# The first layer's attention, issued item by item beside the weight chunks instead of as a stage of its own

## The reference, cut to what matters

```python
def even_mixer(h, w_in, lq1, lk1, lq2, lk2, sub_g, sinks, w_out, lambda_init):
    proj = h @ w_in                      # 2048 -> 4352
    qa, ka, va, qs, ks, vs = jnp.split(proj, idx, axis=-1)
    a_out = diff_attention(qa, ka, va, lq1, lk1, lq2, lk2, sub_g, lambda_init)
    b_out = swa_with_sinks(qs, ks, vs, sinks)
    return jnp.concatenate([a_out, b_out], axis=-1) @ w_out
```

## Time and profile before

| | us |
|---|---|
| median of three runs | 3366.43 (3366.3 to 3367.06) |
| the profiled execution's own time | 3365.45 |
| its span in the trace | 3363.7 |
| busy in it: TensorE, VectorE, ScalarE, GpSimd | 3254.8, 1887.4, 1589.8, 263.5 |

### The profile page before, as it was taken

One profiled execution on the slowest core, in us unless ns is written; L12 is line 12 of the kernel. 1 busy time (PEld: TensorE's weight loads), 2 busy tenths in 40 slices (PEclk: granted clock), 3 DMA queues, 4 the chain that ended last, 5 costly groups with the idle time before them and its releaser, 6 DMA issues.

```text
span 3363.7 us, 39873 instructions
## 1 busy us (share of the span) xinstructions
PE 3254.8 (97%) x15175; PEld 2679.0 (80%) x15175; DVE 1887.4 (56%) x2128; ACT 1589.8 (47%) x2186; POOL 263.5 (8%) x335
## 2 busy tenths in 40 slices
PE   8988999999999999999999999999989999999998
PEld 6866878888888787778888888878778888888886
DVE  4465555554555567755555555557876555554445
ACT  5445454444444467645444445553354543444343
POOL 0001000000000001000460003630000000000000
PEclk9975989999999999989999999989999999999999
DMA  6630545656565455546565556656535665665663
GB/s 229 188 111 7 187 145 189 191 186 191 187 190 185 152 182 163 170 144 200 189 192 190 188 188 218 233 183 203 168 131 168 180 190 194 190 191 189 193 192 116
DMA packets 321365, 595.44 MB, mean 177 GB/s; under 512 B 32612, under 2 KB 39828, under 8 KB 320936
## 3 DMA queue, kind: packets, MB, share of 16 engines
q1 hardware_dynamic: 321192, 593.04, 56.2%
HBM read 581.96 MB, written 11.01 MB: 176 GB/s over the span
## 4 chain that ended last, share of the span: by engine, by line
PE 89%; DVE 6%; ACT 3%; issue 1%; SPq 0%; DMA 0%; ACTq 0%; DVEq 0%
PE pair L1683 27%; PE pair L1685 27%; PE pair L1684 27%; DVE lo L1031 2%; PE turn_ps L1714 1%; ACT hi L575 1%; PE pair L1912 1%; PE turn_ps L1896 1%; PE turn_ps L1838 0%; PE pair L1985 0%; PE misc_ps L1812 0%; PE pair L1838 0%; PE pair L1986 0%; PE pair L1885 0%; DVE conv_o L1136 0%
## 5 line engine op out<-in xcount | busy, mean ns | idle before, releaser
L1031 DVE TENSOR_TENSOR lo<-raw,hi 128x1024 fp32r<-128x1024 f32 x1084 | 1340.2, 1240 | 1291.1 <-ACT hi L575 1280.4
L575 ACT ACTIVATE hi<-raw 128x1024 fp32r<-128x1024 f32 x1084 | 1144.7, 1060 | 1416.0 <-PE pair L1685 1394.2
L1683 PE MATMUL pair<-hi,xt_h 128*128 128x512 f32 (+1 forms) x2784 | 1096.6, 394 | 16.1 <-DVE lo L1031 7.1
L1685 PE MATMUL pair<-lo,xt_h 128*128 128x512 f32 (+1 forms) x2784 | 1086.1, 390 | 0.0
L1684 PE MATMUL pair<-hi,xt_l 128*128 128x512 f32 (+1 forms) x2784 | 1085.5, 390 | 0.0
L1683 PEld LDWEIGHTS pair<-hi,xt_h 128*128 128x128 f32 x2784 | 526.7, 189 | 134.2 <-DVE lo L1031 10.1
L1685 PEld LDWEIGHTS pair<-lo,xt_h 128*128 128x128 f32 x2784 | 525.9, 189 | 109.8
L1684 PEld LDWEIGHTS pair<-hi,xt_l 128*128 128x128 f32 x2784 | 526.6, 189 | 105.2
L1683 PE MATMUL pair<-hi,ht_h 128*128 128x512 f32 x1504 | 587.8, 391 | 4.9 <-DVE ht_l L1145 3.6
L1685 PE MATMUL pair<-lo,ht_h 128*128 128x512 f32 x1504 | 585.4, 389 | 0.0
L1684 PE MATMUL pair<-hi,ht_l 128*128 128x512 f32 x1504 | 585.2, 389 | 0.0
(11 more groups left out here) (279 smaller groups left out, 1745.5 us busy)
## 6 DMA issues: line engine op xcount, KB each, us to landing
raw<-in_mlp_w SPq DMA_DIRECT2D x512, 512.0 KB, 4.1
raw<-in_w_gate SPq DMA_DIRECT2D x88, 512.0 KB, 4.1
raw<-in_w_up SPq DMA_DIRECT2D x88, 512.0 KB, 4.1
raw<-in_w_down SPq DMA_DIRECT2D x88, 512.0 KB, 3.9
raw<-in_even_w_in SPq DMA_DIRECT2D x68, 512.0 KB, 4.4
raw<-in_odd_w_in SPq DMA_DIRECT2D x64, 512.0 KB, 4.0
raw<-in_w_in SPq DMA_DIRECT2D x64, 512.0 KB, 3.9
raw<-in_even_w_out SPq DMA_DIRECT2D x32, 512.0 KB, 4.1
```

The source lines that it names most:

```text
L575: nc.scalar.activation(hi[:, r], raw[:, slot], ACT.Copy).then_inc(sems["hi_ready"], 1)
L1031: nc.vector.tensor_tensor(lo[:, r], raw[:, slot], hi[:, r].bitcast(F32), ALU.subtract).then_inc(sems["lo_ready"], 1)
L1683: nc.tensor.matmul(to, xh[:, t0 + k, tok], h[:, k], start=s, stop=False)
L1685: mm = nc.tensor.matmul(to, xh[:, t0 + k, tok], l[:, k], start=False, stop=e)
```

## The change

The two calls of `attention` and the `drain` are gone. The 32 items, window items first, are issued by a new `heads_at(slot)` beside the chunks, one every second slot from slot 16 on, and one slot later from item 24 on. The input chunks run in the order 6, 8, 7, 0, 2, 4, 1, 3, 5, 68 units in slots 0 to 67. Scores are issued one slot before an item's own, then follow bias (0), exps and probabilities (1), scaling of a window item and the turn (2), copy (3), product (4), out of PSUM (5). Scores have one PSUM buffer (`pair[1]`), turns and products one bank each of `misc_ps`. A window item's probabilities are divided by their sum on ScalarE before the turn, and its product has the values as the stationary operand, so that its output has features on the partitions; it goes into `qk0` in place of its queries. Differential outputs go into `o_diff` with tokens on the partitions. Their heads are normed in three batches (four pairs, two, two): root on ScalarE, reciprocal and product on VectorE, turn on TensorE, hi and lo from PSUM with the gain `subg` as a column.

The output projection is now eight chunks of four units: four with the window half of the weights' rows, set into `acc` in slots 68 to 83, then four with the differential half, added to it. The window half waits for `split_window`, four pairs of roundings and subtractions behind the last input unit; the differential half waits for the batches in turn. Items 24 to 31 run beside the window half.

```diff
-                    64 if kind == "window" else P)
+        FIRST, OUT_WIN, OUT_DIFF = 16, 68, 84
+        HEADS = ([("window", pr, m) for pr in range(8) for m in range(M)]
+                 + [("diff", pr, m) for pr in range(8) for m in range(M)])
+        BATCHES = ((0, 4, 0), (4, 6, 0), (6, 8, 2))
+
+        def head_step(slot, after):
+            k = (slot - after - FIRST) // 2
+            if k >= 24:
+                k = (slot - after - FIRST - 1) // 2
+            late = k >= 24
+            return k if 0 <= k < 32 and FIRST + 2 * k + late + after == slot else None
+
+        def batch_step(slot, after):
+            for b, (_, end, _) in enumerate(BATCHES):
+                k = 16 + 2 * end - 1
+                if FIRST + 2 * k + (k >= 24) + 5 + after == slot:
+                    return b
+            return None
+
+        def roots(b):
+            return stat[:, SUB:SUB + 16].rearrange("p (m h) -> p m h", m=M)[:, :, BATCHES[b][0]:BATCHES[b][1]]
...
-                    self.unit(w_even_in[:, KU * k:KU * k + KU, 0:CH])
+                    self.unit(w_even_in[:, KU * k:KU * k + KU, 6 * CH:7 * CH])
                 for dst, src in (
                     (grows[0:8], i["post_mix_g"].rearrange("l (c n) -> (l c) n", n=CH)),
...
-                    (subg[:], i["even_subln_g"].partition_broadcast(P)),
+                    (subg[:], i["even_subln_g"].rearrange("a p -> p a")),
...
+            def heads_at(self, slot):
+
+                if slot == 13:
+                    self.eng.wait_ge(sems["lam_dot"], 1)
...
+                if b is not None:
+                    self.eng.wait_ge(sems["a_out"], 16 + 2 * BATCHES[b][1])
+                    nc.scalar.activation(roots(b), roots(b), ACT.Sqrt, scale=1.0 / P, bias=eps_col
+                                         ).then_inc(sems["o_root"], 1)
+                k = head_step(slot, 1)
+                if k is not None:
+                    self.head_exp(k)
+                k = head_step(slot, 2)
+                if k is not None and k < 16:
+                    self.head_scale(k)
+                b = batch_step(slot, 2)
+                if b is not None:
+                    self.batch_hi(b)
+
...
+            def head_out(self, k):
+                kind, pr, m = HEADS[k]
+                self.eng.wait_ge(sems["a_mixed"], k + 1)
+                mixed = misc_ps[:, 1, 0:P]
+                if kind == "window":
+                    a = nc.scalar.activation(qk0[:, 16 + pr, m * P:(m + 1) * P], mixed, ACT.Copy)
+                else:
+                    nc.scalar.activation(junk[:], mixed, ACT.Square, accum_out=st(SUB + 8 * m + pr))
+                    a = nc.scalar.activation(o_diff[:, m, pr * P:(pr + 1) * P], mixed, ACT.Copy)
+                a.then_inc(sems["a_out"], 1)
+
+            def batch_hi(self, b):
+                a, e, at = BATCHES[b]
+                self.eng.wait_ge(sems["o_turned"], b + 1)
+                nc.scalar.activation(xt_h[:, a:e], turn_ps[:, at:at + e - a], ACT.Copy, scale=subg[:]
+                                     ).then_inc(sems["o_hi"], 1)
+
+            def split_window(self):
+
+                self.eng.wait_ge(sems["unit_used"], self.T.at("pe"))
+                self.eng.wait_ge(sems["a_out"], 16)
+                for n in range(4):
+                    nc.scalar.activation(xt_h[:, 8 + 2 * n:10 + 2 * n], qk0[:, 16 + 2 * n:18 + 2 * n], ACT.Copy
+                                         ).then_inc(sems["w_hi"], 1)
...
+            def heads_at(self, slot):
+
+                if slot == 12:
+                    self.head_constants()
+                if slot == 14:
+                    self.eng.wait_ge(sems["lam_exp"], self.T.add("lam_exp"))
+                    nc.vector.scalar_tensor_tensor(st(LAM), st(LAMS + 1), -LAMBDA_INIT, st(LAMS), ALU.add, ALU.subtract
+                                                   ).then_inc(sems["dve_step"], 1)
+                    self.eng.wait_ge(sems["dve_step"], self.T.add("dve_step"))
+                k = head_step(slot, 3)
+                if k is not None:
+                    self.head_copy(k)
+                k = head_step(slot, 0)
+                if k is not None:
+                    self.head_bias(k)
+                b = batch_step(slot, 1)
+                if b is not None:
+                    self.batch_norm(b)
+                k = head_step(slot, 1)
+                if k is not None:
+                    self.head_probs(k)
+                b = batch_step(slot, 2)
+                if b is not None:
+                    self.batch_lo(b)
+
...
+            def batch_norm(self, b):
+                a, e, _ = BATCHES[b]
+                self.eng.wait_ge(sems["o_root"], b + 1)
+                nc.vector.reciprocal(roots(b), roots(b)).then_inc(sems["dve_step"], 1)
+                self.eng.wait_ge(sems["dve_step"], self.T.add("dve_step"))
+                for m in range(M):
+                    o = o_diff[:, m, a * P:e * P].rearrange("p (h d) -> p h d", d=P)
+                    factors = st(SUB + 8 * m + a, e - a).unsqueeze(2).to_broadcast([P, e - a, P])
+                    ins = nc.vector.tensor_tensor(o, o, factors, ALU.mult)
+                ins.then_inc(sems["o_normed"], 1)
+
+            def batch_lo(self, b):
+                a, e, at = BATCHES[b]
+                self.eng.wait_ge(sems["o_hi"], b + 1)
+                nc.vector.scalar_tensor_tensor(xt_l[:, a:e], turn_ps[:, at:at + e - a], subg[:],
+                                               xt_h[:, a:e].bitcast(F32), ALU.mult, ALU.subtract
+                                               ).then_inc(sems["o_lo"], 1)
+
+            def split_window(self):
+
+                for n in range(4):
+                    t = 8 + 2 * n
+                    self.eng.wait_ge(sems["w_hi"], n + 1)
+                    nc.vector.tensor_tensor(xt_l[:, t:t + 2], qk0[:, 16 + 2 * n:18 + 2 * n],
+                                            xt_h[:, t:t + 2].bitcast(F32), ALU.subtract).then_inc(sems["w_lo"], 1)
 
...
             def part_wait(self, ready, j, m):
                 if ready == "z" and m == 0:
                     self.eng.wait_ge(sems["z_lo"], j + 1)
+                if ready == "window" and m == 0:
+                    self.eng.wait_ge(sems["w_lo"], j + 1)
+                if ready == "diff" and m == 0:
+                    self.eng.wait_ge(sems["o_lo"], max(1, j))
                 if ready == "mix":
                     self.eng.wait_ge(sems["d_lo"], 2 * j + 1 + m)
-
...
+            def heads_at(self, slot):
+                k = head_step(slot, 4)
+                if k is not None:
+                    self.head_mix(k)
+                k = head_step(slot, 2)
+                if k is not None:
+                    self.head_turn(k)
+                k = head_step(slot, -1)
+                if k is not None:
+                    self.head_scores(k)
+                b = batch_step(slot, 1)
+                if b is not None:
+                    self.batch_turn(b)
+
...
+            def head_mix(self, k):
+                kind, pr, m = HEADS[k]
+                self.eng.wait_ge(sems["a_copied"], k + 1)
+                if k:
+                    self.eng.wait_ge(sems["a_out"], k)
+                if k in (16, 24):
+                    self.eng.wait_ge(sems["psum_free_act"], self.T.at("psum_free_act", int(k == 16)))
...
+            def batch_turn(self, b):
+                a, e, at = BATCHES[b]
+                self.eng.wait_ge(sems["o_normed"], b + 1)
+                if b:
+                    self.eng.wait_ge(sems["o_lo"], 1)
+                else:
+                    self.eng.wait_ge(sems["split_done"], self.T.at("split_done"))
+                for pr in range(a, e):
+                    for m in range(M):
+                        ins = nc.tensor.transpose(turn_ps[:, at + pr - a, m * P:(m + 1) * P],
+                                                  o_diff[:, m, pr * P:(pr + 1) * P], ident[:])
+                ins.then_inc(sems["o_turned"], 1)
 
...
 
             prev = None
-            for c in range(9):
+            for c, at in ((6, 0), (8, 8), (7, 12), (0, 20), (2, 28), (4, 36), (1, 44), (3, 52), (5, 60)):
                 w = (w_even_in, 0, c * CH)
                 if c in (4, 5):
-                    prev = e.chunk("tokens", w, x=XT, prev=prev, dst=v0[:, :, (c - 4) * CH:(c - 3) * CH], more=True)
+                    prev = e.chunk("tokens", w, x=XT, prev=prev, dst=v0[:, :, (c - 4) * CH:(c - 3) * CH], more=True,
+                                   slot1=at)
                 elif c == 8:
-                    prev = e.chunk("kv", w, x=XT, prev=prev, units=4, width=SEQ, to=(None, k_swa[:], 2))
+                    prev = e.chunk("kv", w, x=XT, prev=prev, units=4, width=SEQ, to=(None, k_swa[:], 2), slot1=at)
                 else:
                     t = 4 * c if c < 4 else 16 + 4 * (c - 6)
-                    prev = e.chunk("copy", w, x=XT, prev=prev, to=(None, qk0[:, t:t + 4]),
```

(14 more changed lines are left out.)

376 lines of the change are left out of this document (147 added, 229 removed).

## The result

The changed kernel takes 3308.55 us, the median of four runs (3304.36 to 3309.89), beside 3366.74 for the kernel before on the same chip: a ratio of 0.9824, with a 95% interval of 0.9807 to 0.9841. That is 58.2 us faster. The forecast was 3314 us, 52.4 us faster, in a range of 3301 to 3333. The profiled execution took 3304.36 us with a span of 3302.6; before it was 3365.45 and 3363.7, so between the profiled executions it is 61.1 us.

The account below looks back on a forecast made before the run. TensorE was taken to bound the kernel, except in the half-clock first-layer attention. Saving 118.3 us and adding 52.6 of TensorE work and 13.3 of waits nets 52.4 off 3365.45: 3313.0, median 3314 us, range 3301 to 3333.

Parts of the forecast that it names:

- The stage and what goes with it: First layer's attention stage, slow products behind it, output projection's turns and next norm's table load go: 118.3 us saved.
- The items: Attention's own TensorE work beside the chunks at full clock: 8 x 3.6 + 8 x 2.7 = 50.4 us added.
- Batch turns and the key chunk's turns: TensorE's 16 turns of normed heads, 1.7 us, and four turns of the key chunk, 0.5 us, added.
- Wait 1: Third unit of a chunk comes 0.3 to 0.5 us late in six chunks behind ScalarE's steps: 3 us.
- Wait 2: Input to output projection: TensorE idles 4.0 us while ScalarE and VectorE finish root, evacuation, hi and lo.
- Wait 3: Behind the idle ahead of the output projection the clock halves for a while: 2.0 us lost.
- Waits 4 and 5: TensorE waits for the norms of the second and third batch of heads: 2.2 and 2.1 us.
- all waits are covered: Rival: only the 52.6 us of TensorE work and perhaps 1 us of boundary come back; 3302 us, chance 0.10.
- A microsecond at every item: Rival: ScalarE's and VectorE's in-order queues run late, each turn waits another 1 us; +32, 3346 us, chance 0.13.
- 4.2 us at every item: Rival: each item's turn idles 2.71 us and loses 1.5 to the clock; 134 us, 3434 us, chance 0.04.
- The flickering clock: Rival: short gaps between fp32 groups halve the clock for a tenth of 285 us; 14 us, 3328, chance 0.06.
- The rule on table switches: Skill's 2.66 us per ScalarE table switch would add 5.4 us for four loads, 3319 us; forecast counted 1.3 each.

Follow-up runs that it names:

- act_plus: Changed kernel with one more unused copy of 1024 elements, 1.06 us, on ScalarE ahead of each item's exps: 3311.61 us, ratio 0.9834.
- presplit: Changed kernel with hi and lo of the first four window tiles made in slots 52 to 56, only the last four split at the passage: 3304.08 us.
- after_again: The changed kernel itself, unchanged, measured once more: 3308.91 us, ratio 0.9832 to the kernel before.
- norm_early: Changed kernel with the second and third batch normed on VectorE one slot earlier, ahead of the subtraction: 3306.78 us, ratio 0.9820.
- grouped: Changed kernel with early norms and early split, plus turns, copies, products, outputs of the first 24 items and first batch one slot later: 3308.95 us, ratio 0.9827.

## Why the prediction was right

**The stage and what goes with it (118.3 us).** Right. The half clock stood in the third and the fourth slice, where the prediction names the third alone. Between 240 and 320 us the clock is 1.00 in the first profile, the root finds its table, and the turns of parts 2 and 3 are gone. The turn of `xres` gives a check of the sum: 118.3 less what is found below (57.6) is 60.7 us, and 59.8 were seen.

**The items (50.4 us).** Right, a little high. 16 x 1.73 + 16 x 1.27 = 48.0, at the lower end that I had given. The dilated items from which I took 1.8 us had slow restarts at the clock's change in them, which these have not.

**Batch turns and the key chunk's turns (1.7 + 0.5).** Right in size: the batch of eight turns took 1.02 in the chain, 0.13 each where I had 0.11. The key chunk's turns were not looked at by themselves.

**Wait 1, the third unit of a chunk (3 us).** Wrong: there is none. Between 60 and 252 us TensorE waits nowhere. In this step I had ScalarE's steps pile up behind the first two units. But in the same stretch ScalarE waited for TensorE at 41 of its roundings, 58.8 us in all, so the order piled nothing up that TensorE needed. act_plus shows that with 1.06 us more in each item no turn of the probabilities waits there; only the scores of one item wait once, 1.4 us.

**Wait 2, the passage (4.0 us).** Right in its mechanism: the order on ScalarE and VectorE was the one forecast. The first `lo` let TensorE start 4.7 us behind the last product (4.94 between the starts less a pitch of 0.23), where I had 4.9. But I had given TensorE 0.9 us of item work and forgot that item 25's scores stand there as well; it was 1.5, so the idle was 3.2. presplit shows that the split is the cause: with half of it made before, the idle is gone.

**Wait 3, the clock behind it (2.0 us).** Wrong as a certainty, and its size was met by luck: nothing in the profiled execution, 2.5 us in after_again, and 1.6 us more behind the second batch, which I had not priced. The trace of the kernel before has a case against the certainty that I didn't look at: behind its idle of 3.60 us, up to 1411.15 us, the clock stays at 1.00.

**Waits 4 and 5, the batches (2.2 and 2.1 us).** Right: 2.0 each. norm_early takes them away by VectorE's order alone, so they came from what stood ahead of the norm: at the third batch the subtraction that waits for its rounding, as forecast; at the second mostly the probabilities, whose exps are behind the root's and the exps' own load, and the subtraction behind them.

So the waits and the clock came to 7.4 us in the profiled execution and about 11.5 in after_again, in place of 13.3. The profiled execution came out 8.6 us under its forecast of 3313.0: 2.4 from the items, 3.0 from the third units, 2.0 from a clock that did not fall and 0.9 from the other waits make 8.3. The forecast of the median was 5.5 us too high. There the items and the third units count alike, and the clock, which took more than its 2.0 us in after_again, hid a part of these two misses. The range of 3301 to 3333 is narrower than its bounds added up, 3298 to 3338 (items 48 to 60, waits 0 to 28); the measured time lies in both.

**The rivals.** That all waits are covered gave 3302 and fell: 7.4 us of waits are there. A microsecond at every item and 4.2 us at every item fell: no item waited before 252 us, and with 1.06 us more of ScalarE one did, once. The flickering clock fell for the 180 us that were looked at beside the input chunks: the windows from 60 to 240 us show 1.00 with fp32 groups between the units throughout. In the Trainium skill (TensorE: Matmul & The Clock Gate, A second HAM failure mode: psum-queue depth-cycling) micro-idles between groups of products make the clock go up and down. Beside the items the trace has no idle of TensorE and no fall, so no run here tests that rule; from 240 to 340 us the clock fell only behind idles of 2.0 us and more.

**The rule on table switches.** In the changed kernel the third batch's load is followed like this:

```profile
286.26 1.28 ACT L839 ACT_TABLE_LOAD   x1
287.55 0.30 ACT L839 ACTIVATE stat<-stat 128x4 f32<-128x4 f32 x1
```

The root starts 0.01 us behind the load of 1.28. The Trainium skill (ScalarE: Activation LUTs, What ACT_TABLE_LOAD costs) has 2.66 us a switch, load and drain; the trace agrees with the load and not with a drain. The loads are not free for that: the one at the passage lies in the chain of the idle of 3.2 us, and the pair at the second batch keeps VectorE idle for 1.59 us. What a batch costs is which instructions stand ahead of its norm, and a table load is one of them where it stands there.

## What to carry to other kernels

A stage with no weights to stream is worth issuing piece by piece beside a stage that is bound by TensorE, as long as the other engines have room; what it then costs is TensorE's own groups at the full clock, here 48 us in place of 115, and the waits that the order leaves, here 7 us and up to 4 more of clock. Look for what is left not in the averages but where an in-order engine has one long instruction ahead of one that TensorE needs: moving a norm by a slot and splitting four tiles early took about 9 us of the 11.5 that after_again's profile had in waits and clock. Keep each idle of TensorE short, since idles of 2.0 to 3.6 us cost the clock's fall as well in some executions here, and moving work later by one slot, as grouped did, can make such an idle.

## What was not expected of the hardware

- The granted clock fell behind an idle of 3.2 us in some executions and not in others of the same kernel, and before it had fallen behind 2.71 us. The waits in both were the same to a tenth of a microsecond, and the difference was 2.5 us. Behind the wait of 2.0 us at the second batch it was the same: 1.6 us in one execution and nothing in another; and behind an idle of 3.60 us that every version has it fell in eight of 14 profiles.
- A group of scores between units has a fixed price of some 0.39 us beside 0.055 us per record of 128 columns (two records a product), and joining groups of different kinds saved none of it where it was looked at: 1.78 us for three kinds in one place, and 1.78 for the same in two.
